# A long convolution for two request groups in one stage, its constant tables as high and low part by GpSimd's converting transfers

## What is computed

```python
def short_conv(u, w, b):
    up = jnp.pad(u, ((0, 0), (1, 1), (0, 0)))
    return up[:, :-2] * w[0] + up[:, 1:-1] * w[1] + up[:, 2:] * w[2] + b

def long_conv(u, k_f, bias):
    length = u.shape[1]
    y = jnp.fft.irfft(jnp.fft.rfft(u, n=2 * length, axis=1) * k_f[None], n=2 * length, axis=1)[:, :length]
    return y + u * bias

def hyena_mixer(u, conv_w, conv_b, k_f, hy_bias):
    v, x1, x2 = jnp.split(short_conv(u, conv_w, conv_b), 3, axis=-1)
    z = x1 * long_conv(v, k_f[:, 0], hy_bias[0])
    return x2 * long_conv(z, k_f[:, 1], hy_bias[1])
```

## Time and profile before

| what | us |
|---|---|
| median of 3 runs | 3824.79 (3819.06 to 4182.57) |
| the profiled execution's own time | 3826.06 |
| its span, first to last instruction | 3824.0 |
| span of the prompt's convolution | 944.1 to 1021.0 |
| span of the sample's convolution | 1021.0 to 1297.8 |

### The profile page before, as it was taken

How to read it: one execution, slowest core, us unless ns; L and a number is a source line. 1 busy time by engine, 2 the same in 40 slices (tenths; PEclk the granted TensorE clock), 3 DMA queues, 4 the chain that set the end, 5 groups by cost and what they waited for, 6 DMA issues and landing times.

```text
span 3824.0 us, 59360 instructions
## 1 busy us (share of the span) xinstructions
PE 3409.9 (89%) x23309; PEld 3160.8 (83%) x23309; DVE 2432.6 (64%) x3209; ACT 1943.9 (51%) x3219; POOL 872.4 (23%) x1106
## 2 busy tenths in 40 slices
PE   4877999896487578499999999999999999999997
PEld 2545888785365367499999999999999999999997
DVE  7665211376777442777777777767777777777776
ACT  2124211265122222367667666666666666766675
POOL 2230200010233022123213213222322322321321
PEclk8878999898598788699999999999999999999999
DMA  3445422441242332588888878788888787887885
GB/s 138 175 156 196 135 98 87 114 131 67 102 146 98 137 129 98 176 269 256 264 259 261 261 257 267 259 254 270 257 263 261 258 263 262 258 263 256 265 291 198
DMA packets 215841, 779.61 MB, mean 204 GB/s; under 512 B 28201, under 2 KB 30633, under 8 KB 211340
## 3 DMA queue, kind: packets, MB, share of 16 engines
q1 hardware_dynamic: 201020, 724.33, 56.8%
q0 software_dynamic: 14544, 51.50, 5.1%
HBM read 715.85 MB, written 59.88 MB: 203 GB/s over the span
## 4 chain that ended last, share of the span: by engine, by line
PE 57%; DVE 2%; ACT 0%; issue 0%; POOL 0%; DMA 0%; ACTq 0%; DVEq 0%; POOLq 0%
PE exp_ps L2428 26%; PE exp_py L2428 13%; PE exp_ps L2430 9%; PE exp_py L2430 5%; PE exp_ps L2427 2%; DVE exp_lo L126 1%; PE exp_ps L2411 0%; PE exp_py L2427 0%; PE exp_pr L2420 0%; PE exp_pp L2421 0%; DVE exp_idx L2001 0%; DVE exp_affT L2003 0%; DVE exp_val L2000 0%; DVE exp_xb L2345 0%; DMA exp_xp<-hidden_rows,exp_next_q 0%
## 5 line engine op out<-in xcount | busy, mean ns | idle before, releaser
L2428 PE MATMUL exp_ps<-exp_xt,exp_hi 128*128 128x320 f32 x5632 | 1445.2, 342 | 2.6 <-DVE exp_xt L2310 1.3
L126 DVE TENSOR_TENSOR exp_lo<-exp_raw,exp_hi 128x1024 fp32r<-128x1024 f32 x1056 | 1369.0, 1329 | 79.2 <-ACT exp_hi L122 76.3
L122 ACT ACTIVATE exp_hi<-exp_raw 128x1024 fp32r<-128x1024 f32 x1056 | 1118.2, 1059 | 421.9 <-PE exp_py L2430 228.6
L2430 PE MATMUL exp_ps<-exp_xt,exp_lo 128*128 128x160 f32 x4928 | 1163.7, 236 | 0.0
L2428 PEld LDWEIGHTS exp_ps<-exp_xt,exp_hi 128*128 128x128 f32 x5632 | 1010.0, 189 | 3.9 <-DVE exp_xt L2310 1.7
L2430 PEld LDWEIGHTS exp_ps<-exp_xt,exp_lo 128*128 128x128 f32 x4928 | 941.1, 191 | 0.0
L2428 PE MATMUL exp_py<-exp_hid,exp_hi 128*128 128x320 f32 x2816 | 755.7, 349 | 0.0
L2430 PE MATMUL exp_py<-exp_hid,exp_lo 128*128 128x160 f32 x2688 | 633.7, 236 | 0.0
L2428 PEld LDWEIGHTS exp_py<-exp_hid,exp_hi 128*128 128x128 f32 x2816 | 527.6, 188 | 1.2
L2179 POOL TENSOR_TENSOR exp_hd<-exp_sl,exp_s 128x160 f32<-128x160 f32 x352 | 285.2, 810 | 1026.3 <-ACT exp_sl L2278 1026.3
L2430 PEld LDWEIGHTS exp_py<-exp_hid,exp_lo 128*128 128x128 f32 x2688 | 513.0, 191 | 0.0
(11 more groups left out here) (444 smaller groups left out, 4675.4 us busy)
## 6 DMA issues: line engine op xcount, KB each, us to landing
exp_raw<-in_w SPq DMA_DIRECT2D x1056, 512.0 KB, 4.7
carry_tiles<-in_w_ada SPq DMA_DIRECT2D x24, 1024.0 KB, 5.2
hys_raw<-in_basis_s SPq DMA_DIRECT2D x32, 512.0 KB
features<-proj_xr SPq DMA_DIRECT2D x20, 640.0 KB, 3.5
proj_raw<-in_w_in SPq DMA_DIRECT2D x24, 512.0 KB
filt_raw<-in_kbasis_s SPq DMA_DIRECT2D x18, 512.0 KB
spectrum_s<-filt_spec SPq DMA_DIRECT2D x34, 256.0 KB, 2.1
hys_kt<-spectrum_s POOLq DMA_DIRECT2D x14, 512.0 KB, 4.1
```

Source lines behind the costliest of these rows:

```text
L122: act.activation(self.hi[:, c % self.ns, :], self.raw[:, c % self.nr, :], ACT.Copy).then_inc(self.hi_done, 1)
L126: dve.tensor_tensor(self.lo[:, c % self.ns, :], self.raw[:, c % self.nr, :], self.hi[:, c % self.ns, :].bitcast(F32), ALU.subtract).then_i ...
L2428: mm = pe.matmul(out[:, 0:2 * CAP], wh, rhs, start=first, stop=last)
L2430: mm = pe.matmul(out[:, 0:CAP], wl, rhs[:, 0:CAP], start=False, stop=False)
```

## The change

- The two convolution stages become one, `hyena(nc, a, g, carry)`, which runs the sample's steps and puts the prompt's transform between the sample's inverse steps, as plain float32 products.
- The short convolution moves into the projection: for a convolution block the PSUM copies go into one buffer `pad`, ScalarE makes the middle tap with the bias, VectorE adds the outer two, and the stored block is already convolved. The convolution blocks are now the third to fourteenth block of the projection.
- The input of the convolution is loaded into `carry.tiles` at the end of attention, the prompt's table too.
- The sample's table is stored in memory as high and low part. GpSimd's transfers bring both into fp32r tiles (`table`, five chunks of two parts); there are no splits of it on ScalarE and VectorE. The source is float32 and the tile fp32r, so these transfers convert.
- The inverse finishes the even halves of all four channel blocks first (`even`), then the odd half of one channel block after the other (`odd`), so that VectorE can finish block 0 while TensorE works on block 1. Even and odd halves have banks of their own that swap between the orders (`near`, `far`).
- The second products of a step have one buffer `pt` instead of two, so the products of a step wait for the combination of the step before. SP loads the spectrum and, in place of the pads, the gates (already convolved).
- The result stays in `carry.tiles`, where mix_and_route reads it; its store and reload are gone.

The core of the diff:

```diff
-QK_ORDER = [0, 4, 1, 5, 2, 6, 3, 7] + list(range(8, NF))
+QK_ORDER = [0, 4] + list(range(8, NF)) + [1, 5, 2, 6, 3, 7]
...
+        self.u = self.tiles[:, 0:4 * T].rearrange("p (c t) -> p c t", c=4)
+        self.basis_p = self.tiles[:, 4 * T:4 * T + CH]
...
+            if is_conv(m):
+                if b == 0:
+                    return [(pad[:, 1:515].rearrange("p (a b) -> p a b", a=2)[:, :, 0:256],
+                             src[:].rearrange("p (a b) -> p a b", a=2))]
+                return [(pad[:, c0 + 2:c0 + 2 + w], src[:, 0:w])]
...
                     st.load(sp, 0, NV + NR + m, weights(NV + NR + m))
+                f = QK_ORDER[m]
+                if is_conv(m):
+                    sp.wait_ge(s_cv, 2 * convs(m) + 2)
+                    for c0, c1 in ((0, TP), (TP, T)):
+                        x0 = c0 + (1 if c0 else 0)
+                        sp.dma_start(g["QKH"][f * 128:(f + 1) * 128, c0:c1],
+                                     stage[m % 2][:, x0:x0 + c1 - c0]).then_inc(s_st[m % 2], 16)
...
                         ins = act.activation(to, part, ACT.Copy)
                     ins.then_inc(s_eva, 1)
+                if is_conv(m):
+                    n = QK_ORDER[m] - 8
+                    if n == 0:
+                        act.wait_ge(s_cw, 16)
+                    act.wait_ge(s_eva, 2 * m + 2)
+                    act.wait_ge(s_evd, m + 1)
+                    act.wait_ge(s_st[m % 2], stored(m - 2))
+                    act.wait_ge(s_sk, keys_stored(m))
+                    act.activation(stage[m % 2], pad[:, 1:T + 2], ACT.Identity, bias=cw[:, n, 3:4],
+                                   scale=cw[:, n, 1:2]).then_inc(s_mid, 1)
...
+                if is_conv(m):
+                    n, x = QK_ORDER[m] - 8, convs(m)
+                    dve.wait_ge(s_mid, x + 1)
+                    out = stage[m % 2]
+                    dve.scalar_tensor_tensor(out, pad[:, 0:T + 1], cw[:, n, 0:1], out, ALU.mult, ALU.add).then_inc(s_cv, 1)
+                    dve.wait_ge(s_cv, 2 * x + 1)
+                    dve.scalar_tensor_tensor(out, pad[:, 2:T + 3], cw[:, n, 2:3], out, ALU.mult, ALU.add).then_inc(s_cv, 1)
...
+            sp.wait_ge(s_kl, 3 * (NH - 1))
+            sp.wait_ge(s_ql, 2 * (NH - 1))
+            sp.wait_ge(s_nm, NTT * (NH - 1))
+            sp.dma_start(carry.u, g["QKH"][2 * DA:2 * DA + DH, :].rearrange("(c p) t -> p c t", p=128)).then_inc(carry.s_u, 16)
+            sp.dma_start(carry.basis_p, a["basis_p"][0]).then_inc(carry.s_bp, 16)
...
+        table = ph.sb("table", [128, NS, 2, CH], F32R)
+        s_tab = [ph.sem(f"table_landed{b}") for b in range(NS)]
...
+            def load_k(n):
+                if n >= 2:
+                    sp.wait_ge(s_prod, n - 1)
+                k = spectrum(n)
+                sp.dma_start(kt[:, n % 2, :, :], k[0:2].rearrange("a p f -> p a f")).then_inc(s_kt[n % 2], 16)
...
+                for j in range(STEPS):
+                    load_k(o * STEPS + j)
+                    if j == 1:
+                        sp.wait_ge(s_tr, (o + 1) * 2 * MT)
+                        sp.dma_start(fold[:, :, TP:T], gates(o, TP, T)).then_inc(s_gs, 16)
+                sp.wait_ge(s_trp, (o + 1) * 2)
+                sp.dma_start(fold[:, :, 0:TP], gates(o, 0, TP)).then_inc(s_gp, 16)
...
+            def load(c):
+                if c >= NS:
+                    pool.wait_ge(s_step, c - NS + 1)
+                for x in range(2):
+                    pool.dma_start(table[:, c % NS, x, :], a["basis_s"][c % NC, x]).then_inc(s_tab[c % NS], 16)
...
+            def combine(n):
+                pool.wait_ge(s_prod, n + 1)
+                q = pr[:, n % 2]
+                pool.tensor_tensor(q[:, 0, :], q[:, 0, :], pt[:, 0, :], ALU.add).then_inc(s_pool, 1)
+                pool.tensor_tensor(q[:, 1, :], q[:, 1, :], pt[:, 1, :], ALU.subtract).then_inc(s_pool, 1)
+
+            for c in range(NS):
+                load(c)
             for o in range(2):
-                load_k(pool, o, 0)
-                load_k(pool, o, 1)
+                c0 = o * NC
                 for j in range(NJ):
-                    n = o * NJ + j
-                    pool.wait_ge(s_prod, n + 1)
-                    pool.tensor_tensor(pr[:, n % 2, 0, :], pr[:, n % 2, 0, :], pr[:, n % 2, 1, :], ALU.add).then_inc(s_pool, 1)
-                    pool.tensor_tensor(pr[:, n % 2, 2, :], pr[:, n % 2, 2, :], pr[:, n % 2, 3, :], ALU.subtract).then_inc(s_pool, 1)
-                    if j + 2 < NJ:
-                        load_k(pool, o, j + 2)
-                for c in range(4):
-                    load_pad(pool, 4 + 4 * o + c)
+                    combine(o * STEPS + j)
+                    load(c0 + NS + j)
+                load(c0 + 13)
+                load(c0 + 14)
+                combine(o * STEPS + NJ)
+                combine(o * STEPS + NJ + 1)
+                load(c0 + 15)
+                if o == 0:
+                    for c in range(NS):
+                        load(NC + c)
...
+            def high(o, j):
+                n = o * STEPS + j
+                act.wait_ge(s_pool, 2 * n + 2)
...
+                for x in range(2):
+                    act.wait_ge(s_trp, 2 * o + x + 1)
+                    act.wait_ge(s_pool, 2 * (o * STEPS + NJ))
+                    act.activation(pt[:, x, :], near(o, x)[:], ACT.Copy).then_inc(s_up, 1)
+                act.wait_ge(s_ip, o + 1)
+                act.activation(pt[:, 0, :], near(o, 2)[:], ACT.Copy).then_inc(s_pcp, 1)
+                act.wait_ge(s_step, used(o, 12))
                 for ct in range(4):
-                    act.activation(pc[:, ct, 0:M], bank[4 + ct][:, 0:M], ACT.Copy).then_inc(s_pc, 1)
+                    act.activation(half(ct), far(o, ct)[:], ACT.Copy).then_inc(s_pc, 1)
...
+            def products(n, ur, us):
+                j = n % STEPS
+                dve.wait_ge(s_kt[n % 2], 16 * (n // 2 + 1))
...
+                if n:
+                    dve.wait_ge(s_pool, 2 * n)
+                k, q = kt[:, n % 2], pr[:, n % 2]
+                dve.tensor_tensor(q[:, 0, :], ur, k[:, 0, :], ALU.mult)
+                dve.tensor_tensor(pt[:, 0, :], us, k[:, 1, :], ALU.mult)
+                dve.tensor_tensor(q[:, 1, :], us, kx[:] if j in (0, NJ) else k[:, 0, :], ALU.mult)
+                dve.tensor_tensor(pt[:, 1, :], ur, k[:, 1, :], ALU.mult).then_inc(s_prod, 1)
...
+            def out_s(o, ct):
+                dve.wait_ge(s_pc, 4 * o + ct + 1)
+                if ct < 3:
+                    dve.wait_ge(s_ct, 3 * o + ct + 1)
+                else:
+                    dve.wait_ge(s_step, used(o, NC))
...
+                    out_s(o, ct)
+                    if o == 0:
+                        fold_s(ct)
...
+            def even(o, i):
+                ready(pe, o * NC + 8 + i)
+                for j in (2 * i, 2 * i + 1):
+                    pe.wait_ge(s_Pl, 2 * (o * NJ + j) + 2)
+                    for ct in range(4):
+                        mm = inverse(o, far(o, ct), ct, j, j // MT, 16 + j)
+                mm.then_inc(s_step, 1)
+
+            def odd(o, ct):
+                for j in range(NJ):
+                    if ct == 0 and j % 2 == 0:
+                        ready(pe, o * NC + 12 + j // 2)
+                    mm = inverse(o, near(o, ct), ct, j, 1 - j // MT, 24 + j)
+                    if ct == 3 and j % 2:
+                        mm.then_inc(s_step, 1)
+                if ct < 3:
+                    mm.then_inc(s_ct, 1)
...
+                    forward(o, j)
+                even(o, 0)
+                prompt_transposes(o)
+                even(o, 1)
+                prompt_forward(o)
+                even(o, 2)
+                even(o, 3)
+                prompt_inverse(o)
+                odd(o, 0)
+                odd(o, 1)
+                pe.wait_ge(s_zp, o + 1)
+                odd(o, 2)
+                odd(o, 3)
...
+        work = carry.tiles
...
         def _(sp):
-            for ct in range(4):
-                sp.dma_start(yh[:, ct, :], g["MIXT"][DA + ct * 128:DA + (ct + 1) * 128, :]).then_inc(s_y[ct], 16)
...
-            for c in range(2):
-                st.split_hi(act, 0, 0, c)
             for ct in range(4):
-                act.wait_ge(s_y[ct], 16)
                 act.activation(raw[:, ct, :], yh[:, ct, :], ACT.Square).then_inc(s_sq, 1)
-            for c in range(2, 8):
+            for c in range(8):
                 st.split_hi(act, 0, 0, c)
...
+    b = np.ascontiguousarray(b, dtype=np.float32)
+    if MT == 4:
+        hi = rounded(b)
+        b = np.stack([hi, rounded(b - hi)], 1)
+    return {f"basis_{s}": b}
```

414 lines of the change are left out of this document (222 added, 192 removed).

## The result

The changed kernel takes 3667.9 us (median of 4 runs, 3665.57 to 3669.73) against 3821.93 before (median of 4): a ratio of 0.9607, with a 95% interval from 0.9582 to 0.9632. One run of before, at 4182.57 us, was a slow one and is not in the ratio. The profiled execution takes 3669.73 us where that of before took 3826.06: 156 us less. The forecast was 126 less, 3700 us, and the range began at 3672: the direction and what bounds the stage were as said, the gain was larger than the range allowed, since TensorE's work in the stage was put too high.

What follows compares the result with a forecast made beforehand. TensorE was taken as the bound, its waits in the 353.7 us of convolution stages as the gain: -121 there, -6 in mix_and_route, +1 in projection, from 3826.06 to 3700 us. The range was 3672 to 3824 us.

Steps and rivals of the forecast that it cites:

- TensorE's work in the joined stage: Joined stage, each order: sample products 89.6 us, prompt 10, one clock loss 2.7, together 102.3 us.
- What bounds the stage: Joined stage: TensorE busy above 0.85; 47.7 us of fold waits shrink, 7.92 us waits between forward and inverse go.
- Clock: Joined stage: one loss of 2.7 us at each order's start, with TensorE at the 1.2 GHz level.
- Prompt's cover and chunks 2 to 4: Joined stage: prompt's products lose 1 us an order despite even chunks as cover; waits for table chunks 2 to 4, 3 us.
- Turn and end: Joined stage: TensorE waits 7 us between orders for the last block alone; the end costs 2.7 plus 3 us.
- The start: Joined stage: 10 us to TensorE's first product, bounds 7 and 15.
- VectorE's loop: Joined stage's forward steps: 5.9 us plus 0.1 against TensorE's 5.6; VectorE's 3 us lag covered by the even chunks.
- Rivals 1, 2 and 4: Table transfers at half pace (3816 us, 0.18), a third (3946, 0.12); GpSimd held until landing (3796, 0.08 with Rival 3).
- The forecast's 4.0 us a chunk: Joined stage: a table chunk of 1.05 MB costs all engines 4.0 us at most, hidden with five chunks.
- Rival 3: Joined stage: TensorE stays at 1.2 GHz, 74 us more, kernel 3774 us; chance 0.08 together with rival 4.
- The rule on GpSimd's descriptors: Joined stage: busy VectorE does not delay GpSimd's descriptors; otherwise 620 ns become 3100, estimate 64 us more.
- mix_and_route, projection, attention: Other stages: mix_and_route -6 us (bounds 0 and 10), projection +1 (0 to 3), attention no term in the sum.

Runs made afterwards that it cites:

- e3: Changed kernel with the table stored as one float32 number and split by ScalarE and VectorE, four chunks: 3693.23 us, ratio 0.9665 to before.
- e7: Changed kernel with four table chunks, each half transferred a second time into an unread fp32r buffer (converting): 3729.58 us, one execution.
- e8: Changed kernel with four table chunks, each half transferred a second time into an unread float32 buffer (plain): 3724.45 us, one execution.
- e2: Changed kernel with four table chunks instead of five, the prompt's combinations issued before chunks 14 and 15: 3677.34 us, one execution.
- e9: Kernel of e3 with both combining operations on VectorE instead of GpSimd: 3676.67 us, ratio 0.9619 to before.
- e6: Changed kernel with the convolution's result stored and reloaded, two w_out splits again ahead of the squares: 3689.46 us, one execution.
- the second pair: The kernel before and the changed kernel, each profiled again without edits: 3820.15 and 3671.86 us.
- e11: The changed kernel, unedited, profiled a second time: 3671.86 us, ratio 0.9600 to before.
- e5: Changed kernel with the odd halves of all four channel blocks gathered together, ready only after the last step: 3692.59 us, one execution.

## Why the prediction was right in kind and too small

The step that failed is TensorE's work in the joined stage, put at 2 x 102.3 us. The first order took 1044.73 - 947.62 = 97.1 us and the second 95.5: 12.0 us less, the largest part of the 20 by which the stage came out shorter. The other parts are waits of TensorE that did not come (5 us) and the start, the turn and the end (3).

- **What bounds the stage.** Right. Of 212.2 us TensorE is busy 202.47, and the waits that were named are those that went: 47.7 to 12.5 us for folds, the two pauses between forward and inverse to none.
- **TensorE's work, 102.3 us an order.** Too high. From the first product of the second order to the place where one more would start, 0.23 us behind the last start, are 1146.35 - 1050.88 = 95.5 us. Two terms of the work itself were mis-sized. A product takes 0.226 to 0.229 us, not 0.233 (three starts, too few for the last digit): at 0.227, 768 products are 4.9 us less. And the prompt is 95.5 - 384 x 0.227 = 8.3 us an order, not 10: 3.4 us together. By its groups the forward products take 7.4 / 2 = 3.7 us for 4.3, the inverse 7.5 / 2 = 3.75 for 4.3, the transposes 1.05 for 1.4. The rate of 2.1 ns a column came from the sums of squares, which begin behind a pause of 29.20 us, in a stretch of that trace with a clock of 0.58 (1297.8 to 1361.4 us); here the clock was full.
- **Clock.** 2.7 us were counted for each order; only the first has a loss (ten starts from 947.62 to 951.36, 0.42 us apart), and it is 97.1 - 95.5 = 1.6 us: 3.8 us less than forecast. Between the orders the transposes leave no pause of more than 1.86 us.
- **Prompt's cover and chunks 2 to 4.** Taken as 2 and 3 us, both 0.
- **Turn and end.** 7 and 5.7 us forecast, 6.2 (1044.73 to 1050.88) and 4.1 measured: 2.4 us. The start was 9.4 for 10. All in all 4.9 + 3.4 + 3.8 + 5 + 2.4 + 0.6 = 20.1 us, which is the miss of the stage, 232.3 - 212.2.
- **VectorE's loop.** 5.9 us and 0.1 for the wait were forecast, 6.06 measured, and no wait of TensorE in the forward steps. What was said of the cover holds only just: in e3 a step of 6.92 us makes TensorE wait from the fifth step on, because its products have banks for two steps. The even chunks cover the last lag, not one that grows in each step.
- **The table.** Rivals 1, 2 and 4 fall on landing in 4.8 us (median), 2.9 us a MB and issues of 0.56 us; e7 and e8 show that converting adds a tenth of a plain transfer's engine time. The forecast's 4.0 us a chunk was high too (3.0), but with five or four chunks (e2) it does not decide. Rival 3 falls on the clock of 0.97.
- **The rule on GpSimd's descriptors.** The issues did not get longer beside VectorE. But the same section of the Trainium skill (SBUF — State Buffer, on its two separate sides) also says that a VectorE instruction with both inputs in SBUF contends with a GpSimd instruction that reads SBUF, and that the later one blocks until the first is done. This is what e3's rows show, 0.68 against 1.77 us and 1.22 against 2.31, and e9, in which it is gone. The prediction weighed the rule for two-port modes only. It took 1.2 us for a split in the projection and left L126's 2.31 us in the earlier trace rows without a word: the split beside GpSimd cost 2.3 us a step. Its loop of 5.9 us came out right because it took GpSimd's 3.36 us from a step in which the same low parts run beside the combinations; without them the two take 2 x 1.28.
- **mix_and_route, projection, attention.** -6 forecast, -7.0 measured, of which e6 gives 5.8 back. Projection +1, measured +0.6. Attention 0, measured +6.8 in one profile and -1.2 in the second pair: its load at the end is hidden, and the rest is scatter. The 13.2 us at the start, which e11 shows to lie within the scatter, and the 6.8 of attention together moved the compared execution 6.4 us downwards. The other 24 us of the miss of 30 stand in stages that repeat: the stage's 20.5, mix_and_route's 1, and small remainders. With e11's profile (3677.73 us) in place of the first the gain would be 148 us, and that execution lies inside the range; the two medians, 3667.9 and 3671.86, lie below its end of 3672, the second by 0.1 us.
- **The range.** Its low end allowed 28 us below the forecast, but named nothing in it for TensorE's work, whose terms were all taken at the upper value; these errors add.

Where the 142 us of the stage come from, by what was undone alone: 20 from the table's split taken off (e3), 22 from finishing block after block (e5, one execution). The remaining 100 are put down to the merging of the prompt's stage, the short convolution moved away and the even banks. That is argued from the waits that are gone, and not shown: these were not undone one by one, and how they share the 100 us is open.

## What to carry to other kernels

Where TensorE is the bound of a merged stage, take its pace from the middle of a long row at full clock, and the price of small float32 products from rows at the same clock level, not from products behind a pause. Where VectorE and GpSimd both work on SBUF at the same time, look at two equal operations of one step: if one takes longer than the other, moving GpSimd's work onto VectorE may be faster than making VectorE's work less (e9: 19 us of the stage for two operations moved). And profile the same kernel twice before a difference of some 10 us in untouched code is given a cause.

## What the runs showed of the hardware that was not expected

- A VectorE subtraction with both inputs on the chip takes 0.68 us for 128x512 and 1.22 for 128x1024; started while GpSimd's `TENSOR_TENSOR` runs, 1.77 and 2.31: the rest of GpSimd's operation and then its own time. GpSimd's operation of 128x512 takes 1.28 us alone and 1.66 to 1.74 when it starts beside such a subtraction. That GpSimd's operations are the cause of VectorE's part is shown by e9; that each wait lasts to the other's end is read from the rows, to within some 0.13 us.
- Converting float32 to fp32r in GpSimd's transfers costs 2.9 us of all engines a MB against 2.6 plain (e7, e8), and changes neither issue (0.54 us) nor landing (6.7 us converting and 6.6 plain, for the second transfers of these two).
- The stretch up to the first copy of the values (the filters and the start of the projection) ends anywhere from 373.3 to 386.9 us, 13.7 us apart in two executions of one kernel, while the joined stage of 212.2 us was 210.6 in the second one. What decides it stays open.
